# A convolution norm with tokens on the partitions, and a new order around it, in a two-block transformer kernel

## The reference, cut to what matters

```python
mem_n = layer_norm(mem, mem_ln_g, mem_ln_b)

q_t = q * jnp.exp(b); k_t = k * jnp.exp(-b)          # b: running sum of log f in chunks of 32
scores = jnp.where(causal, einsum(q_t, k_t), 0.0)
k_end = k * jnp.exp(b_last - b)                       # feeds the states of the chunks
...
o = o * lax.rsqrt(jnp.mean(jnp.square(o), axis=-1, keepdims=True) + RMS_EPS)
o = o.reshape(...) * hg_norm_g * jax.nn.silu(g)
u = conv(a * jax.nn.sigmoid(a_gate)) + cv_b           # 31 taps, each channel by itself
u = jax.nn.silu(layer_norm(u, cv_ln_g, cv_ln_b))      # over the 512 channels
return jnp.concatenate([o, u], -1) @ w_out            # 1024 x 1024
```

## Time and profile before

| | us |
|---|---|
| median of 3 runs (lowest, highest) | 1360.31 (1359.61, 1360.40) |
| profiled execution | 1359.01 |
| its span, first to last instruction | 1356.8 |
| TensorE busy | 1289.7 (95% of the span) |
| VectorE busy | 874.7 (64%) |
| ScalarE busy | 664.6 (49%) |
| mean granted TensorE clock | 0.983 of full |

### The profile page before, as it was taken

The page is one execution under the profiler, slowest core; times in us unless marked ns, Lnnn a source line. Parts: engine busy times, 40 slices in busy tenths (PEclk is TensorE's granted clock), DMA queues, the critical chain, the costliest instruction groups (busy, mean ns, idle before and its releaser), DMA issues.

```text
span 1356.8 us, 18071 instructions
## 1 busy us (share of the span) xinstructions
PE 1289.7 (95%) x7188; PEld 1117.1 (82%) x7188; DVE 874.7 (64%) x1432; ACT 664.6 (49%) x994; POOL 5.2 (0%) x7
## 2 busy tenths in 40 slices
PE   8899999999999999999787899999999999999997
PEld 7788888897788888899775797788888997788886
DVE  5565557878677565679996565545557665545555
ACT  5554446666564444555523454543444654543443
POOL 0000000000000000000000000000001000000000
PEclk9899999999999999999897999999999999999999
DMA  7455555542455555454421442555554442455551
GB/s 277 140 186 188 189 181 187 184 143 78 132 171 186 189 187 191 148 171 158 154 69 58 170 132 86 187 180 177 186 188 160 167 135 83 155 180 177 187 187 61
DMA packets 61571, 215.84 MB, mean 159 GB/s; under 512 B 6576, under 2 KB 9904, under 8 KB 61232
## 3 DMA queue, kind: packets, MB, share of 16 engines
q1 hardware_dynamic: 61056, 213.15, 47.5%
q10 hardware_dynamic: 432, 1.54, 0.4%
HBM read 213.62 MB, written 1.05 MB: 158 GB/s over the span
## 4 chain that ended last, share of the span: by engine, by line
PE 79%; DVE 14%; ACT 4%; issue 1%; DMA 0%; SPq 0%; ACTq 0%; DVEq 0%
PE bank L1816 24%; PE bank L1818 23%; PE bank L1817 23%; DVE w_lo L1013 3%; DVE arena L1645 3%; PE bank L1996 1%; PE bank L1883 1%; ACT w_hi L507 1%; PE bank L2094 1%; PE bank L2134 1%; ACT xs L646 1%; DVE xs L1712 1%; PE bank L2105 1%; DVE rt L1063 0%; DMA w_raw<-weights_d 0%
## 5 line engine op out<-in xcount | busy, mean ns | idle before, releaser
L1013 DVE TENSOR_TENSOR w_lo<-w_raw,w_hi 128x1024 fp32r<-128x1024 f32 x395 | 482.1, 1225 | 380.5 <-ACT w_hi L507 379.0
L507 ACT ACTIVATE w_hi<-w_raw 128x1024 fp32r<-128x1024 f32 x395 | 416.7, 1059 | 553.8 <-PE bank L1818 546.8
L1816 PE MATMUL bank<-w_hi,x_hi 128*128 128x512 f32 (+2 forms) x992 | 374.6, 378 | 14.2 <-DVE x_lo L1031 7.7
L1818 PE MATMUL bank<-w_hi,x_lo 128*128 128x512 f32 (+2 forms) x992 | 368.9, 372 | 0.0
L1817 PE MATMUL bank<-w_lo,x_hi 128*128 128x512 f32 (+2 forms) x992 | 368.8, 372 | 0.0
L1816 PEld LDWEIGHTS bank<-w_hi,x_hi 128*128 128x128 f32 x992 | 188.4, 190 | 50.5 <-issue 11.8
L1818 PEld LDWEIGHTS bank<-w_hi,x_lo 128*128 128x128 f32 x992 | 187.9, 189 | 32.1
L1817 PEld LDWEIGHTS bank<-w_lo,x_hi 128*128 128x128 f32 x992 | 188.3, 190 | 30.6
L1816 PE MATMUL bank<-w_hi,h_hi 128*128 128x512 f32 (+1 forms) x364 | 142.3, 391 | 0.0
L1818 PE MATMUL bank<-w_hi,h_lo 128*128 128x512 f32 (+1 forms) x364 | 141.3, 388 | 0.0
L1817 PE MATMUL bank<-w_lo,h_hi 128*128 128x512 f32 (+1 forms) x364 | 141.3, 388 | 0.0
(11 more groups left out here) (308 smaller groups left out, 1393.1 us busy)
## 6 DMA issues: line engine op xcount, KB each, us to landing
w_raw<-weights_d SPq DMA_DIRECT2D x395, 512.0 KB, 3.3
arena<-weights_d SPq DMA_DIRECT2D x4, 512.0 KB, 5.8
arena<-late_d SPq DMA_DIRECT2D x1, 1056.0 KB, 5.9
xs<-x_d SPq DMA_DIRECT2D x2, 512.0 KB, 6.2
kv_mem<-mem_d ACTq DMA_DIRECT2D x1, 1024.0 KB, 6.8
out_d<-xs SPq DMA_DIRECT2D x4, 256.0 KB, 2.8
cst<-cst_d SPq DMA_DIRECT2D x1, 671.0 KB, 10.3
arena<-pT_d ACTq DMA_DIRECT2D x1, 256.0 KB, 2.6
```

What stands on the lines that cost most here:

```text
L507: nc.scalar.activation(w_hi[:, b % RING, :], w_raw[:, b % RAW, :], ACT.Copy).then_inc(hi_ready, 1)
L1013: nc.vector.tensor_tensor(w_lo[:, b % RING, :], w_raw[:, b % RAW, :], w_hi[:, b % RING, :].bitcast(F32), ALU.subtract).then_inc(lo_ready, 1)
L1816: nc.tensor.matmul(out, wh, xh, start=start, stop=False, skip_group_check=True)
L1818: return nc.tensor.matmul(out, wl, xh, start=False, stop=stop, skip_group_check=True)
```

## The change

1. VectorE's memory statistics move to just after the first gate (`gated(0)`), ahead of the splits of blocks 8 to 11. ScalarE's `memory_norm` moves to just after the split behind up-block 2.
2. VectorE forms `kt` at n = 15 and `hq` at n = 16. The masking of the scores moves ahead of the splits of n = 18 and n = 19. Eleven taps fewer stand in the twenty steps (79 for 90); they come out in the final `conv_taps`, after the last state. The scores wait for `hk_ready` 2, ScalarE's L911 for 3.
3. The recurrence's squares are summed as columns: eight products of a 128x128 stationary square with one column of ones give 128x8. The root is taken there, eight diagonal matrices are made (four by ScalarE, four by VectorE), and eight products with ones spread them.
4. The convolution is transposed (eight transposes) into two banks, its mean and variance are taken by `bn_stats`, the root on 128x2, ScalarE normalises token half 0 and VectorE half 1, eight transposes turn it back, and `conv_norm` reads it from the bank.
5. TensorE runs memory blocks 3 and 4 before the spreading, block 5 after it. VectorE's splits behind memory blocks 4 and 5 stand after the recurrence's `x_lo`.
6. `AB_OUT` becomes (0,0) (0,1) (1,0) (0,2) (0,3), then (1,1) (1,2) (1,3), and the second half's banks become 0 and 1.

```diff
-AB_OUT = tuple((h, j) for h in range(2) for j in range(4))
-XA_OUT = ((0, 0), (0, 1), (1, 0), (0, 2), (0, 3), (1, 1), (1, 2), (1, 3))
+AB_OUT = XA_OUT = ((0, 0), (0, 1), (1, 0), (0, 2), (0, 3), (1, 1), (1, 2), (1, 3))
...
-        Z_BANK = {5: ((2, 3), (4, 5)), 6: ((6, 7), (0, 1)), 7: ((4, 5), (6, 7)), 8: ((6, 0), (7, 1)), 9: ((6, 7), (0, 1)),
+        Z_BANK = {5: ((2, 3), (0, 1)), 6: ((6, 7), (0, 1)), 7: ((4, 5), (6, 7)), 8: ((6, 0), (7, 1)), 9: ((6, 7), (0, 1)),
...
                 for i in range(4):
                     behind(b1 + ffn_place("U", 0, i))
+                    if f == 0 and i == 2:
+                        memory_norm()
...
                 gated(0)
+                if f == 0:
+                    memory_stats()
...
                 behind(b1 + ffn_place("U", 0, 3))
-                if f == 0:
-                    memory_stats()
...
-                    act.wait_ge(hk_ready, 2)
+                    act.wait_ge(hk_ready, 3)
...
-            for c in range(CC):
-                act.wait_ge(conv_done, c + 1)
-                nc.scalar.activation(xs[:, c, 1, :], conv[:, c, :], ACT.Square).then_inc(conv_sq, 1)
-            mem_blocks(1, 3, 6)
+            act.wait_ge(ho_root, 1)
+            for i in range(HG_HEADS):
+                nc.scalar.activation(ho_dg[:, i, :], ident, ACT.Copy, scale=ho_rc[:, i:i + 1]).then_inc(ho_da, 1)
+            mem_blocks(1, 3, 4)
+            act.wait_ge(conv_stat, 1)
+            nc.scalar.activation(x_part(0, 0, 1), quarters(PB[2][:, :]), ACT.Identity, scale=ln_r[:, 0:1], bias=ln_m[:, 0:1]
+                                 ).then_inc(conv_na, 1)
+            mem_blocks(1, 4, 6)
...
-            beside = {1: 9, 3: 11, 5: 11, 7: 5, 8: 6, 9: 6, 10: 6, 11: 6, 12: 6, 13: 1, 14: 6, 15: 6, 16: 0, 17: 3, 18: 4, 19: 4}
+            beside = {1: 9, 3: 11, 5: 11, 7: 5, 8: 6, 9: 6, 10: 5, 11: 5, 12: 4, 13: 1, 14: 4, 15: 2, 16: 0, 17: 2, 18: 4, 19: 4}
             for n in range(20):
+                if n == 18:
+                    masked_scores()
                 blk()
...
+                if n == 15:
                     dve.wait_ge(e_ready, 2)
                     dve.wait_ge(k_ready, HG_HEADS)
                     nc.vector.tensor_tensor(kt[:, :, :], kt[:, :, :], hk[:, :, :], ALU.mult).then_inc(hk_ready, 1)
+                if n == 16:
+                    dve.wait_ge(q_evac, HG_HEADS)
+                    nc.vector.tensor_tensor(hq[:, :, :], hq[:, :, :], eb[:, :, :], ALU.mult).then_inc(hk_ready, 1)
+                    dve.wait_ge(hk_ready, 2)
+                    nc.vector.tensor_tensor(eb_g, b_last, b_g, ALU.subtract).then_inc(hk_ready, 1)
...
+            dve.wait_ge(ho_sum, 1)
+            link(nc.vector.tensor_scalar(rv[:, 0:2 * HG_HEADS], PB[0][:, 0:2 * HG_HEADS], 1.0 / P, RMS_EPS, ALU.mult, ALU.add))
+            rsqrt(ho_rc, rv[:, 0:2 * HG_HEADS]).then_inc(ho_root, 1)
+            dve.wait_ge(ho_root, 1)
+            for i in range(HG_HEADS, 2 * HG_HEADS):
+                nc.vector.tensor_scalar(ho_dg[:, i, :], ident, ho_rc[:, i:i + 1], None, ALU.mult).then_inc(ho_dd, 1)
+
+            dve.wait_ge(conv_ps, 1)
+            for t in range(2):
+                mark(nc.vector.bn_stats(ln_bn[t][:, 0:6], PB[2 + t][:, :]))
...
+            link(rsqrt(ln_r, ln_var))
+            nc.vector.tensor_scalar(ln_m[:, 0:1], ln_mv[0][:, 0:1], ln_r[:, 0:1], -1.0, ALU.mult, ALU.mult).then_inc(conv_stat, 1)
+            nc.vector.tensor_scalar(x_part(0, 1, 1), quarters(PB[3][:, :]), ln_mv[1][:, 0:1], ln_r[:, 1:2], ALU.subtract, ALU.mult
+                                    ).then_inc(conv_nd, 1)
             mem_blocks(3, 4)
-
-            dve.wait_ge(conv_stat, 1)
-            ln_sums(3, CV_CH, rstd[:])
-            dve.wait_ge(ho_stat, 1)
-            link(nc.vector.tensor_scalar(rv[0:32, S:2 * S], PB[0][0:32, 0:S], 1.0 / P, RMS_EPS, ALU.mult, ALU.add))
-            rsqrt(rlat[:], rv[:]).then_inc(ho_rows, 1)
-            dve.wait_ge(ho_rows, 1)
-            link(nc.vector.scalar_tensor_tensor(rstd[:], rstd[:], -1.0, rlat[:, 0:S], ALU.mult, ALU.mult))
-            for c in range(0, CC, 2):
-                centre(conv, c, rlat[:, 0:S], rstd[:], conv_t)
-            mem_blocks(4, 5)
...
+            for h in range(HG_HEADS):
+                pe.wait_ge(ho_sq, h + 1)
+                for t in range(2):
+                    ins = nc.tensor.matmul(PB[0][:, 2 * h + t:2 * h + t + 1], ho_sq_buf[:, h, t * P:(t + 1) * P], ones[:, 0:1],
+                                           start=True, stop=True)
+            ins.then_inc(ho_sum, 1)
             for c in range(CC):
                 pe.wait_ge(conv_done, c + 1)
-                nc.tensor.matmul(half(3, 0), ones, conv[:, c, :], start=c == 0, stop=c == CC - 1)
+                for t in range(2):
+                    ins = nc.tensor.transpose(PB[2 + t][:, c * P:(c + 1) * P], conv[:, c, t * P:(t + 1) * P], ident)
+            ins.then_inc(conv_ps, 1)
+            pe.wait_ge(g_silu, HG_HEADS)
+            mem_blocks(1, 3, 5)
+            pe.wait_ge(ho_da, HG_HEADS)
+            for i in range(2 * HG_HEADS):
+                if i == HG_HEADS:
+                    pe.wait_ge(ho_dd, HG_HEADS)
+                h = i // 2
+                ins = nc.tensor.matmul(half(1 - h // 2, h)[:, i % 2 * P:i % 2 * P + P], ones, ho_dg[:, i, :], start=True, stop=True)
+                if i % 4 == 3:
+                    ins.then_inc(ho_bc, 1)
+            mem_blocks(1, 5, 6)
+            pe.wait_ge(conv_na, 1)
+            pe.wait_ge(conv_nd, 1)
             for c in range(CC):
...
+                for t in range(2):
+                    ins = nc.tensor.transpose(half(4 + c // 2, c)[:, t * P:(t + 1) * P], xs[:, c, 1, t * P:(t + 1) * P], ident)
+                if c % 2:
+                    ins.then_inc(conv_t, 1)
             pe.wait_ge(id_scaled, 1)
             token_out(5, AB_OUT, "ab_out", lambda c: pe.wait_ge(hy_lo, c + 1) if c < 4 else pe.wait_ge(cy_lo, c - 3), lambda i: None)
```

More of the change, by code:

```diff
@@ L945, in _ @@
                 nc.scalar.activation(x_hi[:, h, :], ho[:, h, :], ACT.Copy).then_inc(hy_hi, 1)
-            for c in range(1, CC):
+            for c in range(CC):
                 conv_norm(c)
@@ L1278, in token_ffn @@
                 nb[0] = b1 + FFN_BLOCKS - 1
[L1280 to L1291, removed]
-                link(nc.vector.tensor_scalar(rv[:, 0:S], rv[:, 0:S], 0.0, LN_EPS, ALU.max, ALU.add))
-            def centre(view, c, r, m, signal):
-                w = view[:, c:c + 2, :]
-                link(nc.vector.tensor_tensor(w, w, bc(r, 2), ALU.mult))
-                for k in range(2):
-                    nc.vector.tensor_tensor(view[:, c + k, :], view[:, c + k, :], m, ALU.add).then_inc(signal, 1)
             def ln_part(v, h, t):
@@ L1683, in _ @@
                 conv_taps(beside.get(n, 0))
-            dve.wait_ge(sc_ps, 1)
-            dve.wait_ge(hk_ready, 4)
-            for t in range(2):
-                mark(nc.vector.tensor_scalar(sc[:, t, :], PB[t][:, :], BIG, -BIG, ALU.min, ALU.max))
-            settle()
-            for t in range(2):
-                s = sc[:, t, :].rearrange("p (h q) -> p h q", q=P)
-                nc.vector.tensor_tensor(s, s, bc(causal, HG_HEADS), ALU.mult).then_inc(sc_ready, 1)
             conv_taps(6)
@@ L2422, in _ @@
-            for c in range(CC):
-                pe.wait_ge(conv_sq, c + 1)
-                ins = nc.tensor.matmul(half(3, 1), ones, xs[:, c, 1, :], start=c == 0, stop=c == CC - 1)
-            ins.then_inc(conv_stat, 1)
-            for h in range(HG_HEADS):
-                pe.wait_ge(ho_sq, h + 1)
-                ins = row_sums(PB[0][0:32, 0:S], "rows_all", h, ho_sq_buf[:, h, :], h == 0, h == HG_HEADS - 1)
-            ins.then_inc(ho_stat, 1)
-            pe.wait_ge(g_silu, HG_HEADS)
-            mem_blocks(1, 3, 6)
@@ L2433, in _ @@
-            pe.wait_ge(ho_rows, 1)
-            for h in range(HG_HEADS):
-                ins = nc.tensor.matmul(half(1 - h // 2, h), spread(h), ho_r, start=True, stop=True)
-                if h % 2:
-                    ins.then_inc(ho_bc, 1)
+                for t in range(2):
+                    ins = nc.tensor.transpose(PB[2 + t][:, c * P:(c + 1) * P], conv[:, c, t * P:(t + 1) * P], ident)
+            ins.then_inc(conv_ps, 1)
+            pe.wait_ge(g_silu, HG_HEADS)
+            mem_blocks(1, 3, 5)
```

49 lines of the change are left out of this document (24 added, 25 removed).

## The result

| | before | after |
|---|---|---|
| median (lowest, highest), us | 1359.96 (1358.19, 1360.40) of 4 | 1341.11 (1340.92, 1341.19) of 4 |
| span of the profiled execution | 1356.8 | 1339.2 |
| mean granted TensorE clock | 0.983 | 0.988 |
| VectorE's first tap starts | 611.95 | 604.81 |
| VectorE's gate products start, right after the last tap | 710.84 | 705.85 |

The ratio is 0.9864, with a 95% interval of 0.9846 to 0.9881: faster by 1.4%. The profiled span fell by 17.6 us: 7.1 before the mixer, 8.6 between the first tap and the projection, 1.9 behind its start.

The account below looks back on a forecast made before the run. TensorE is busy 95% of the span, so gains lie in its waits and low-clock stretches; VectorE's list sets the mixer's pace. Memory 7.0 plus mixer and tail 12.2 give 19.2 us, so 1341.1 us; range 1336 to 1349.

Parts of the forecast that it names:

- Memory: First feed-forward: earlier statistics remove a 4.76 us wait and 1.6 and 1.3 of low clock, less 0.7 new wait: 7.0 us.
- The rival of a wait at each of blocks 8 to 11: First feed-forward: TensorE held at each block, so the memory part gives only 0 to 2 us; 1347; chance 0.14.
- Scores: Mixer: TensorE starts the scores at 663.0, not 668.05, after a 0.8 us wait, at the full clock.
- First states: Mixer: the first state chain on VectorE ends at 681.2, 4.0 us earlier.
- VectorE loses about 0.5 beside it: Mixer: head's products at low clock take 5.2 us beside VectorE's 5.0 of own work, costing VectorE about 0.5.
- From the gate products to the projection: Tail: convolution ends at 711.3, projection starts at 726.8, not 737.04.
- Projection's first block at the full level: Output projection: after a wait of only 1.5 us TensorE keeps the full clock, saving 2.0 us.
- The rival of a clock that stays low through the tail: Tail and first projection blocks, 711 to 725, at the lower level: 7.3 us gain, 1353; chance 0.10.
- Slower by a masking that waits for the scores: VectorE's masking at n = 18 waits for late scores, delaying the stage; a loss from d = 21.3 us; chance 0.03.
- A sign of being wrong that it named: Mixer: the prediction is wrong if taps after the last state take longer than 8 us.
- The bounds: Memory gain 4.1 to 7.7 us, tail gain 8.0 to 14.5; taken singly, 1337.5 to 1346.
- that the states come no earlier, for 1345: Mixer: VectorE's list too full, so only memory and tail gain without the 4.0: 15.2 us; chance within full gain's 0.70.

Follow-up runs that it names:

- the controls: The changed kernel unchanged, run again in the second and third groups: 1343.43 us (ratio 0.9885) and 1343.96 us (0.9892).
- the three groups: Twelve follow-up runs, each group sharing its runs of the kernel before: medians 1358.64, 1358.85 and 1357.72 us.
- The twenty products: Changed kernel plus 20 unread products of ones on TensorE before the wait for the first head's states: 1342.98 us, ratio 0.9881.
- the first control: The changed kernel unchanged, run again in the second group: 1343.43 us (1340.93 to 1344.28), ratio 0.9885.
- block 5 late: Changed kernel with memory block 5 moved behind the eight transposes back, in all three engines' lists: 1340.93 us, ratio 0.9868.
- block 5 late with the old list: Changed kernel with memory block 5 behind the transposes back and VectorE's mixer list as in the kernel before: 1340.16 us, ratio 0.9860.
- the version with the old list: Changed kernel with VectorE's mixer list (taps, kt, hq, masking) as before, new tail kept: 1342.98 us (1338.01 to 1347.40), ratio 0.9883.
- block 5 late and filled: Changed kernel with memory block 5 behind the transposes back and 20 unread products before the wait for head 0's states: 1340.77 us, ratio 0.9865.

## Why the prediction was right, and where it was off

The forecast was 1341.1 and the median 1341.11. That closeness is partly luck: the span fell by 17.6 us and not by 19.2, the median before was taken 1.3 us above its profiled execution, and the controls of the same program gave 1343.4 and 1344.0. Against the kernel before the three groups give 18.9, 15.4 and 13.8 us, all at or below the 19.2 forecast. The mechanism and the order of the terms held. Step by step, forecast and measured:

- **Memory: 7.0, measured 7.14.** New wait 0.7, was 1.08 (0.5 to 0.6 in three other profiles). The 16 transposes and the two groups behind them at the full level: 1.7 and 1.36, were 1.67 (44.87 to 46.54) and 1.47. The rival of a wait at each of blocks 8 to 11 is out: there is one wait, and the run with this part alone is 6.3 us faster.
- **Scores** at the full level after a wait of 0.8: 0.76, clock 1.00. **First states** 4.0 earlier: 4.0. **Wait for them** 6.8: 6.81, lower level behind it as forecast.
- **VectorE loses about 0.5 beside it: measured 1.8.** This is the term that failed. For the next head's product the 0.5 was right (0.48). What the step left out is the second place where the slow TensorE holds VectorE, a split whose `w_hi` comes late (1.32). It priced only the head's products at the lower level and took the full level to be back 4 to 6 us after each restart; behind this wait it came back after 8.5 us (674.21 to 682.7), and the gate block that frees the buffer ran at half speed too. The twenty products in the wait make both go. So the last states came 2.5 us earlier instead of 4.0 (4.0 - 1.8, and 0.4 from four taps that take 1.66 in place of 2.04), and all behind them some 1.5 late. In five other profiles a third such wait of 1.4 us follows, so the result's profile is a kind one.
- **From the gate products to the projection: forecast 15.5 (711.3 to 726.8), measured 15.48.** Inside it, terms differ both ways: blocks 3 and 4 end 7.75 after the wait (forecast 7.9, though its own terms, 0.3, 5.8 and 2.0, add up to 8.1); the spreading took 0.21 for each product (713.74 to 715.44 for eight), where I took 0.27 from a pair with a latency in it; from the start of `x_hi` to the projection it is 1.45 (forecast 0.9). The wait before the projection is 1.9 (forecast 1.5). VectorE's chain from the gate products to the gain products is 10.54 (forecast 10.6). For a spreading product the Trainium skill's four passes for true float32 (FP8 and Floating Point Precision, section TensorE Precision Notes) gave an estimated 0.21 us; the trace agrees (0.21).
- **Projection's first block at the full level: forecast 2.0, measured 1.9.** The rival of a clock that stays low through the tail is out for this stretch: the window 720 to 724 shows 1.00. In part it is in: the wait of 3.4 cost 1.7 (forecast 2.0).
- **The order costs and gives nothing:** the run without it shows no difference in the stage (16.2 and 619.1, where the first control has 16.2 and 619.0).
- **Slower by a masking that waits for the scores:** VectorE starts the masking at 660.17 without a wait.
- **A sign of being wrong that it named:** more than 8 us of taps after the last state, where its sum has 8.0 with the split. From the end of the last states to the gate products it is 8.08 us in the result's profile and 9.6 in the first control, by the third wait. That sign was on the line, and it points at the same failed step.
- **The bounds:** taken singly, those of the memory part and of the tail give 1338.8 to 1345.3, not 1337.5 to 1346.

The sum is then 7.14 + 8.57 (start of the projection, forecast 10.2) + 1.9 = 17.6, all of the span's difference. That the last term fits so well is luck in part: with the same first block at the full level, the controls have 619.0 and 616.4 us behind the projection's start. One thing the prediction had among its rivals in the wrong form: that the states come no earlier, for 1345. What happens is that the states do come earlier and the time does not need them; the 8.6 us are 10.7 from the new tail less 2.1 that the moved taps cost in front of it. By the profile with block 5 late, the old VectorE list would have been as good or better. That it is better in time was not shown.

What stays open: whether the old list has an advantage in time, how the clock chooses its places, and what each part of the new tail (the columns, the transposed convolution, the order of the memory blocks) is worth by itself; no run takes them apart. The version with the lowest median and the lowest run is block 5 late with the old list, 1340.16 us; whether its median is below the one with the new list can't be told.

## What to carry to other kernels

When work is moved from before a milestone to after it, write down what the stage behind waits for: the states came earlier and the convolution later, and by the traces it was the convolution that counted. Where two chains meet, a filler block belongs behind the last work that the slower chain needs: block 5 ahead of eight transposes and of ScalarE's `x_hi` cost some 2 to 3 us. Price a stretch at the lower clock at every point where another engine waits for TensorE, the ring's buffers included.

## What the runs showed of the hardware

- The changed kernel's runs differ by 5 us (1340.9 to 1346.1), those of the version with the old list by 9 (1338.0 to 1347.4); the fastest have mean clocks of 0.988 and 0.991, the slowest both 0.983. All three profiles of the changed kernel show the lower level around the wait of 6.8 us and around the one for the last taps (3.4, in the first control 2.4), but other places come and go. TensorE is busy for 1.1 of the 4 us from 592 to 596 in both runs compared here; the granted clock of 596 to 600 is 1.00 in the result's profile and 0.69 in the run with block 5 late and filled:

```profile
596.00:600.00 4.00, 4.00 (x26) 4.00 (x25) 3.42 (x10) 0.53 (x2) 0.00 (x0) 0.69 0.37 120
```

- The lower level also comes without a wait of several us. In the changed kernel the last wait ahead of this stretch is one of 1.24 us, which ends at 690.78; whether the wait is its cause is not shown:

```profile
692.00:696.00 4.00, 4.00 (x32) 3.74 (x32) 3.93 (x10) 0.66 (x2) 0.00 (x0) 0.61 0.38 122
```

- It even comes while TensorE is busy without a break. In the first control TensorE waits for nothing from 690.38 to 704.6 us; the clock is 0.99 from 699 to 702 and falls behind that:

```profile
690.38:704.60 14.22, 14.22 (x96) 13.58 (x96) 12.44 (x29) 2.82 (x7) 0.00 (x0) 0.69 0.21 75
702.00:704.00 2.00, 2.00 (x13) 2.00 (x13) 1.89 (x6) 0.00 (x0) 0.00 (x0) 0.62 0.64 244
```

- The reciprocal roots on 128x8 and on 128x2 took 2.2 us each (eleven steps of 0.20, four times the width at no cost), and ScalarE's four 128x128 copies with a scale column start 0.30 apart (709.6 to 710.5). A product with one column of ones takes 0.22, as much as one of 128 columns (0.21).
